# Some TensorE transposes of an encoder layer done by DMA transposes instead

## What is computed

```python
def encoder_layer(x, ...):
    x = x + 0.5 * swiglu(rms_norm(x, ffn1_norm), ffn1_w_gate, ffn1_w_up, ffn1_w_down)
    z = rms_norm(x, mix_norm) @ w_in
    b_gate, c_gate, h, q_lat, kv_lat, k_rope_raw = jnp.split(z, cuts, axis=-1)
    y_conv = short_conv_mixer(b_gate, c_gate, h, conv_w)
    y_att = latent_attention(q_lat, kv_lat, k_rope_raw, ...)      # 8 heads, no mask
    x = x + jnp.concatenate([y_conv, y_att], axis=-1) @ w_out
    x = x + 0.5 * swiglu(rms_norm(x, ffn2_norm), ffn2_w_gate, ffn2_w_up, ffn2_w_down)
    return x        # then a final rms_norm

def swiglu(x, w_gate, w_up, w_down):
    return (jax.nn.silu(x @ w_gate) * (x @ w_up)) @ w_down
```

## Time and profile before

| | us |
|---|---|
| median of 3 runs | 4522.36 |
| lowest, highest of them | 4517.55, 4590.06 |
| the profiled execution's own time | 4518.26 |
| its span on the slowest core (core 2) | 4517.0 |
| span of the other seven cores | 4510.3 to 4514.9 |

### The profile page before, as it was taken

How to read it: one execution, slowest core, us unless ns; L and a number is a source line. 1 busy time by engine, 2 the same in 40 slices (tenths; PEclk the granted TensorE clock), 3 DMA queues, 4 the chain that set the end, 5 groups by cost and what they waited for, 6 DMA issues and landing times.

```text
span 4517.0 us, 78649 instructions; the slowest of 8 cores (4510.3 to 4517.0 us)
## 1 busy us (share of the span) xinstructions
PE 4408.2 (98%) x30719; PEld 2263.3 (50%) x31256; DVE 1273.2 (28%) x2268; ACT 2144.7 (47%) x3054; POOL 267.8 (6%) x473
## 2 busy tenths in 40 slices
PE   7999999999999999899999999999999999999999
PEld 4444444444444555456666665565444444444444
DVE  2222222222222665322222222233222222222222
ACT  2122222222222765599999999995222222222221
POOL 1000000000000222200000000000000000000000
PEclk9999999999999999999999999999999999999999
DMA  9533333333214885642221214335111111111110
GB/s 176 114 83 81 82 80 82 80 82 82 68 57 149 209 207 136 150 114 75 80 74 67 75 54 158 109 108 177 57 56 57 57 56 57 56 57 56 56 58 27
DMA packets 146204, 413.29 MB, mean 91 GB/s; under 512 B 23088, under 2 KB 42864, under 8 KB 142768
## 3 DMA queue, kind: packets, MB, share of 16 engines
q1 hardware_dynamic: 94032, 245.37, 17.3%
q0 software_dynamic: 51808, 162.87, 15.1%
HBM read 336.75 MB, written 145.53 MB: 107 GB/s over the span
## 4 chain that ended last, share of the span: by engine, by line
PE 86%; ACT 5%; issue 4%; DMA 3%; DVE 1%; POOL 0%; DVEq 0%; ACTq 0%; SPq 0%; POOLq 0%
PE ps L384 20%; PE ps L314 19%; PE ps L311 19%; PE ps L1437 10%; PE ps L1460 5%; ACT a_P L1444 4%; PE ps L796 3%; PE tp L1339 2%; DMA f1wg<-ffn_w_gate 2%; PE tp L1255 2%; PE ps L726 1%; PE tp L288 1%; DMA f1wd<-ffn_w_down 1%; PE ps L729 1%; PE ps L936 1%
## 5 line engine op out<-in xcount | busy, mean ns | idle before, releaser
L1444 ACT ACTIVATE a_P<-ps 128x1024 bf16<-128x1024 f32 x1280 | 1186.5, 1067 | 11.2 <-PE ps L1437 7.4
L1437 PE MATMUL ps<-a_QT,a_KT 112*128 112x512 bf16 x2560 | 769.4, 382 | 25.9 <-ACT a_P L1444 5.0
L1460 PEld LDWEIGHTS ps<-a_V,a_P 128*128 128x128 bf16 x10240 | 485.3, 97 | 306.6 <-issue 1.8
L1460 PE MATMUL ps<-a_V,a_P 128*128 128x65 bf16 x10240 | 523.6, 194 | 0.5 <-ACT a_P L1444 0.5
L311 PE MATMUL ps<-f2xnT,f2wg 128*128 128x512 bf16 x2065 | 494.6, 379 | 3.9 <-ACT f2xnT L295 1.4
L311 PE MATMUL ps<-f1xnT,f1wg 128*128 128x512 bf16 x2059 | 494.1, 380 | 3.8 <-ACT f1xmT L295 0.7
L314 PE MATMUL ps<-f1xnT,f1wu 128*128 128x512 bf16 x2076 | 495.2, 379 | 1.9
L314 PE MATMUL ps<-f2xnT,f2wu 128*128 128x512 bf16 x2075 | 495.0, 379 | 1.9
L329 ACT ACTIVATE f1stmp<-ps 128x512 f32<-128x512 f32 x264 | 157.6, 597 | 700.1 <-PE ps L314 700.0
L329 ACT ACTIVATE f2stmp<-ps 128x512 f32<-128x512 f32 x264 | 157.6, 597 | 693.0 <-PE ps L314 690.0
L384 PE MATMUL ps<-f1wd,f1hT 128*128 128x512 bf16 x2063 | 460.4, 380 | 11.9 <-DMA f1wd<-ffn_w_down 7.6
(11 more groups left out here) (168 smaller groups left out, 3294.1 us busy)
## 6 DMA issues: line engine op xcount, KB each, us to landing
f1res<-xin SPq DMA_DIRECT2D x50, 512.0 KB, 4.7
f2res<-x_d SPq DMA_DIRECT2D x50, 512.0 KB, 4.4
x_d<-f1res POOLq DMA_DIRECT2D x48, 512.0 KB, 4.5
m_xin<-x_d SPq DMA_DIRECT2D x48, 512.0 KB, 5.3
a_x<-x_d SPq DMA_DIRECT2D x48, 512.0 KB, 3.3
x_d<-a_x POOLq DMA_DIRECT2D x48, 512.0 KB, 3.4
y<-f2res POOLq DMA_DIRECT2D x48, 512.0 KB, 2.9
f1xin<-xin SPq DMA_DIRECT2D x46, 512.0 KB, 3.8
```

What stands on the lines that cost most here:

```text
L1437: ins = nc.tensor.matmul(sbank[:, j * 512:(j + 1) * 512], lhsT=KT[h][:, kt * 128:(kt + 1) * 128], rhs=QT[qc % 2][:, h, :], start=True, sto ...
L1444: ins = nc.scalar.activation(out=Pb[:, pi % NPB, :], in_=sbank, func=AF.Exp, scale=SCALE)
L1460: ins = nc.tensor.matmul(ob[:, qs, :], lhsT=Pb[:, pi % NPB, j * 512 + qs * 128:j * 512 + (qs + 1) * 128], rhs=V[h][:, kt0 + j, :], start=( ...
```

## The change

For every row group of tiles 1 to 11 of both FFN phases, `xpose` issues one DMA transpose from SP (128 x 1024, `xn` to `xnT`) and returns: no TensorE transposes and no ACT copy. SP waits for the norm of that group and for the matmuls that last read that `xnT` buffer. `square(x)` then waits for the DMA transpose of x-2, and `gate_up(t)` waits on TensorE for the DMA transposes of groups 2 and 3. Tile 0 of each phase and the meta rows stay on TensorE.

In attention the outputs of tiles 0 to 6 (`NTD = 7`) are transposed by four DMA transposes each (128 x 512, `yk` to `yT`, `o_tr_dma`) at the same places of the plan; tiles 7 to 11 stay as they were. The first matmul of an `o_mm` group waits for all four. In tile 7's plan (which works on tile 6's output) the `o_mm` matmuls are strewn over 96 blocks from `at + 24` on, where they lay over 72 blocks from `at + 9` on. Some semaphores are made only where they are used.

```diff
@@ square
             if x >= 2:
-                W(nc.scalar, s_tp, tp_n[x - 2])
+                WT(nc.scalar, tr_n.get(x - 2) or (s_tp, tp_n[x - 2]))
@@ xpose
             t, s, _, rows = subs[x]
+            if t >= 1:
+                W(nc.sync, s_xn, x + 1)
+                if t >= 2:
+                    W(nc.sync, s_g, g_end[t - 2])
+                s_tr.sig(x % 2, nc.sync.dma_start_transpose(out=xnT[t % 2][:, :, s * 128:s * 128 + 128],
+                                                            in_=xn[:, x % 2, :]))
+                tr_n[x] = (s_tr.s[x % 2], s_tr.s[x % 2].n)
+                return
             W(nc.tensor, s_xn, x + 1)
...
             W(nc.scalar, s_tp, tp_n[x])
-            if t >= 2:
-                W(nc.scalar, s_g, g_end[t - 2])
@@ gate_up
-            W(nc.tensor, s_tc, tc_n[at[(t, 3)]])
+            if t == 0:
+                W(nc.tensor, s_tc, tc_n[at[(t, 3)]])
+            else:
+                WT(nc.tensor, tr_n[at[(t, 2)]])
+                WT(nc.tensor, tr_n[at[(t, 3)]])
@@ ch_mm
-            W(nc.tensor, s_yc, s_yc.n)
@@ attn_phase
+    def o_tr_dma(tile, a):
+
+        if a == 0:
+            W(nc.sync, s_nm, 8 * (tile + 1))
+            W(nc.sync, s_gm, o_end.get(tile - 1, 0))
+        s_yd.sig(nc.sync.dma_start_transpose(out=yT[:, :, a * 128:(a + 1) * 128], in_=yk[:, tile % 2, a, :]), 16)
+
@@ o_mm
-            W(nc.tensor, s_yc, 2 * tile + (1 if i == 0 and tile >= 7 else 2))
+            if tile < NTD:
+                W(nc.tensor, s_yd, 64 * (tile + 1))
+            else:
+                W(nc.tensor, s_yc, 2 * (tile - NTD) + (1 if i == 0 else 2))
@@ plan
-            steps += [(at + 4 + a, lambda a=a: o_tr(tile - 1, a)) for a in range(4)]
+            tr = o_tr_dma if tile - 1 < NTD else o_tr
+            steps += [(at + 4 + a, lambda a=a: tr(tile - 1, a)) for a in range(4)]
...
-        b0, nb_ = (66, 60) if tile == 0 else (at + 9, 119 if nxt else 72 if tile == 7 else 56)
+        b0, nb_ = (66, 60) if tile == 0 else (at + 24, 96) if tile == 7 else (at + 9, 119 if nxt else 56)
@@ norm (attention)
         if h == 0:
-            W(nc.vector, s_yt, 2 * (qc - 1))
+            W(nc.vector, s_yd, 64 * min(qc - 1, NTD))
+            W(nc.vector, s_yt, 2 * (qc - 1 - NTD))
```

## The result

The changed kernel takes 4479.7, 4479.7 and 4482.0 us (mean 4480.4), against 4517.6 and 4522.4 us (mean 4520.0) for the kernel before: a ratio of 0.9913, 95% interval [0.9884, 0.9941]. The forecast was 4477 with a range of 4468 to 4560. Some executions were disturbed, with one die at a lower granted clock; all numbers here leave them out, and where a die was disturbed in a profiled execution its rows come from a core of the other die.

What follows compares the result with a forecast made beforehand. TensorE, busy 98% of the span, was taken as the bound, with ACT in attention. Gains of 39.4 us (FFN) and 1.7 us (attention), DMA transposes hidden at cost 0, came off 4518.3 us: 4477, range 4468 to 4560.

Steps and rivals of the forecast that it cites:

- The gain in the FFN: FFN down projections: removing TensorE's transposes saves 1.79 us a tile over 22 tiles, 39.4 us.
- Attention's gain: Attention: ACT's gap of 0.24 us behind the transposes goes in seven tiles, 1.7 us; upper end 11.2 us.
- The landing: FFN's fourth DMA transpose, behind two loads on SP: lands 5.7 us after issue, so hidden at cost 0.
- the lower end: Landing estimate for the FFN transpose: two loads first, then 256 KB moved like them, 4.3 us after issue.
- The window: FFN2, fourth transpose's issue to the gate's weights load: 8.3 us, or about 10.6 if the norm comes earlier.
- The ring of two row buffers: FFN: `square(x)` waits for the transpose of x-2, issued over 9.5 us earlier and long landed; no cost.
- Late at the gate: Rival: fourth transpose lands after 8.3 to 14 us, TensorE waits at 22 gates; 4536 us at 11 us; 11%.
- Late in attention: Rival: attention's four transposes go one by one, 3.9 us late in seven tiles, ACT runs dry; 4504 us; 6%.
- SP's queue: Rival: FFN transposes hold SP's queue over 4.7 us, delaying input loads and norms; about 4850 us at 9.5; 16%.
- the break-even of 1.9 us a tile: FFN gates: a TensorE wait of 1.9 us at each of 22 gates would cancel the 41.1 us gain.
- costs nothing: Attention: moving tile 6's projection by 15 blocks costs nothing; it ends at block 120 of 130.

Runs made afterwards that it cites:

- e1: Changed kernel with only the FFN part of the change, attention as in the kernel before: 4479.9 us, ratio to before 0.9916.
- e3: Changed kernel without the FFN's DMA transposes of tiles 2 to 11 (80 of 88 left out): 4477.4 us, ratio to before 0.991.
- e10: Changed kernel with the `a_xT` load earlier and each FFN transpose issued ahead of its two loads on SP: ratio to before 0.9909.
- e7: Changed kernel with the `a_xT` load earlier and three of four row blocks of mixing-stage tiles 1 to 11 transposed by DMA: ratio to before 0.9954.
- e9: Changed kernel with only the fourth DMA transpose of each FFN tile done three times, each after the last landed: ratio to before 1.005.
- e5: Changed kernel with every FFN DMA transpose done twice, the second after the first landed: ratio to before 1.0184.
- e11: Changed kernel with the edits of e10 and e9 together: ratio to before 0.9978.
- e6: Changed kernel with every FFN DMA transpose done three times, each after the last landed: ratio to before 1.0864.
- e8: Changed kernel with attention's tiles 7 to 10 also transposed by DMA and the output projection's plan not moved for them: ratio to before 0.9972.
- e12: Changed kernel with attention's tile 7 plan put back, tile 6's output projection 15 slots earlier, its rows still transposed by DMA: ratio to before 0.9926.

## Why the prediction was right, and where it was not

**The gain in the FFN** was 39.4 us in the sum. The tile came out as worked out (37.98 us against 37.99, gate to gate 4358.24 - 4244.28 = 113.96 against 113.9), and e1 alone measured 37.9 us. The starts of FFN2's down projection, before and after, give the same for the whole phase (first and last start, us):

```profile
L384 PE MATMUL ps<-f2wd,f2hT x2065: 379/379/379, 3197.2 to 4508.2; 128*128 128x512 bf16 x188
...
L397 PE MATMUL ps<-f2wd,f2hT x2112: 379/379/379, 3180.7 to 4472.0; 128*128 128x512 bf16 x192
```

1311.0 us became 1291.3, on every core to 0.1: 19.7 us, eleven times 1.79. FFN1 from its second tile on went from 1273.3 to 1255.4, ten times 1.79. In the one tile left, FFN1's first, the gain is not seen: its down projection takes 57.0 to 59.7 us on the eight cores before and 55.9 to 59.0 after, since TensorE also waits for that projection's weights there, 4.7 to 7.6 us before and 6.9 to 9.4 after.

**Attention's gain** of 1.7 us was there, somewhat larger, and the changed kernel lost most of it again. The exponentials' first and last start, before, in the changed kernel and in e3, whose attention is the changed kernel's and where no core waits for `a_xT`:

```profile
L1444 ACT ACTIVATE a_P<-ps x1280: 1018/1058/1135, 1879.4 to 3097.9; 128x1024 bf16<-128x1024 f32 x183
...
L1472 ACT ACTIVATE a_P<-ps x1280: 1018/1058/1133, 1860.5 to 3081.0; 128x1024 bf16<-128x1024 f32 x183
...
L1473 ACT ACTIVATE a_P<-ps x1280: 1017/1055/1133, 1860.9 to 3076.0; 128x1024 bf16<-128x1024 f32 x183
```

These are 1218.5, 1220.5 and 1215.1 us. Over the eight cores the stretch is 1216.4 to 1218.5 us before, 1217.8 to 1218.4 in e1, which has attention as before, 1213.7 to 1215.2 in e3 and 1215.3 to 1220.5 in the changed kernel. So the transposes' part is worth about 3 us, and the wait for `a_xT`, which no step of the prediction had, takes most of it back, all of it on the slowest core. That and FFN1's first tile are where the traces show the forecast's miss of some 3 us (4480.4 against 4477).

**The landing** was taken as 5.7 us and measured 5.6, but the step behind it was wrong, and that the figures agree is luck. I took a 256 KB store in pieces as the nearest row. The transpose itself takes 2.7 us and its two predecessors 2.9 (e10). The sum that I had called the lower end, loads first and then a short transfer, was the right construction; its terms were too small by 1.3 us, 0.7 of it because the residual load lands in 5.1 us after the change and not in 4.4. A page of the profile that lists landings by median gives a latency together with the queue of that place; e7's 8.1 us are the same operation. The prediction named a landing past 10 us, or a hold of SP past 5, as a sign of being wrong. Both came at the first transpose of FFN1 (11.3 and 5.7 us) and cost nothing, because it is not the fourth of its tile; every other landing in the FFN of that core was below 9 us.

The Trainium skill, in VectorE: DVE Perf Modes, The three transpose paths, gives 1309 ns for a 128 x 128 transpose by DMA. Here eight of them took 2.7 us, at most 0.34 us each. The same page of the Trainium skill, in Rules for kernel authors, advises TensorE where a destination in PSUM will do. In this FFN, where TensorE had no time to spare, the DMA was the better choice by 1.79 us a tile.

**The window** failed in its second half. The narrower one, 8.3 us, was measured at 8.5 (7.2 in e9's tile). The wider one, 10.6, did not come in FFN2. The norm did come earlier, 12.8 us before the gate instead of 11.4, but the residual load ahead of the transpose waits for a store to `y`, an event of the output side that I had not looked at. I followed the engines' order and not that of SP's queue.

**The ring of two row buffers** was dismissed in half a sentence ("long landed"). In FFN1 ACT does wait on it, 22 times and 125.4 us in all:

```profile
who waited for it (us, times):
  ACT f1xn L271: 125.4, 22
```

It costs nothing (e3, with 2 such waits instead of 22, has FFN1 at the same 1255.5 us); e5 and e7 show what it costs when the transposes are slower. The step was wrong and its cover was real.

**The rivals.** *Late at the gate*: no wait at all on any core; e9 shows the mechanism and a corrected price. Where waits and lengthening are read from the FFN stretches of one core, a microsecond of TensorE's wait cost 1.4 to 1.5 us (126 / 90.8 in e5, 71 / 50.3 in e9, 38 / 26.2 in e11, 435 / 296.5 in e6). I had priced it at 1.0; the break-even of 1.9 us a tile is rather 1.3. *Late in attention*: e8 and e12 show it where the plan is not moved, so "costs nothing" was right for the move and would have been wrong for leaving it out. *SP's queue*: SP is held for 1.24 us by a transpose (median), not 4.7. e5 holds it for about 8 us a block in the FFN1 tile shown and was 1.8% slower than before, near the 2% that I had put at 6.7 us. In FFN1 that went through ACT and the row buffers, but in FFN2, with one input buffer, it went through the input loads, as the rival has it. ACT's waits for them, before, after and in e5:

```profile
ACT f2xn L268 <- DMA f2xin<-x_d: 17.7, 11, 2.6
...
ACT f2xn L271 <- DMA f2xin<-x_d: 104.2, 33, 6.3
...
ACT f2xn L271 <- DMA f2xin<-x_d: 148.6, 33, 6.8
```

So this rival's first sign, ACT waiting for the input load of three groups in every tile, is already there in the changed kernel (ACT also comes to that wait earlier, without its copies); what is absent is a fourth transpose that is late at the gate. That the rival had 16% was the price of having no row for the hold.

What stays open: why `a_xT` comes later after the change (34.5 us from issue to landing on core 6, 32.9 before). The eight cores reach attention somewhat closer together (first exponential 1860.2 to 1862.9 us, 1876.1 to 1880.2 before), and more loads at once could do it, but no run tests that.

## What to carry to other kernels

A transpose moved from a saturated TensorE to the DMA engines is worth its issue time in TensorE's stream, not its listed duration, and in this kernel cost nothing as long as its landing stayed inside the slack of the first engine that waited for it, which can be ACT waiting for a row buffer and not TensorE. Look also at the loads that stand behind it in its queue. Read that slack in several tiles and cores, from the last item ahead of it in its queue, and price a wait that falls on TensorE at more than itself. Where the DMA engines are busy, or the consumer's plan is earlier than the landing, leave the transpose on TensorE or move the plan.

## What the hardware showed that was not expected

- A DMA transpose of 128 x 1024 bf16 held SP for 1.24 us (median; longest 5.7; plain loads of 512 KB beside it: 0.32 and 0.33), landed in 2.7 us with nothing ahead of it, 5.6 behind two loads, and 8.1 (longest 21.0) where the DMA engines were 80% busy.
- After a stop TensorE's matmuls ran at about half speed: eight in 3.57 us instead of 1.89 after 6.44 us (e5), one in 0.63 instead of 0.38 after 9.82 us (e8). The granted clock was 0.50 in the 5 us after either stop, which is 1.2 GHz of the two levels, 1.2 and 2.4 GHz. The mean granted clock of the whole stretch fell from 1.00 to 0.99 in e8 and to 0.96 in e7. The Trainium skill, in TensorE: Matmul & The Clock Gate, Part 1, says that an idle array is held at half its clock until activity releases it; these rows agree.
